# First-block queries and keys projected by tokens, head norms in token layout, convolution taps dealt anew, and the recurrence's constants moved to the start

## The chip, the cores and the metric

The kernel runs on one core of a Trainium2 chip. The metric is the device time of one execution, in microseconds, as the median of several executions. All data is float32. A matrix product is done on TensorE in a rounded 32-bit form (fp32r), with three products for one: each operand is split into a high and a low part.

## The reference

Two transformer blocks over 256 tokens of width 1024, one after the other.

```python
def first_block(x, mem, ...):
    h, mem_h = rms_norm(x, norm_g), rms_norm(mem, mem_norm_g)
    c_glu, c_gate, d_q, d_k, d_v, d_gate, x_q, x_gate, merge = split(h @ w_in)
    y_conv = conformer_conv_branch(c_glu, c_gate, ...)   # 31 taps, layer norm, silu, projection
    y_diff = differential_attention_branch(d_q, d_k, d_v, d_gate, ...)   # 8 heads of 2 x 64
    y_mem = memory_cross_attention_branch(x_q, x_gate, mem_h, ...)       # 4 heads of 256
    g = sigmoid(merge)
    return x + (g[0] * y_conv + g[1] * y_diff + g[2] * y_mem) @ w_out

q = rms_norm(q.reshape(B, S, H, 2, d), qn_g)        # d = 64, over each half head; k likewise
q = rms_norm(q.reshape(B, S, X_HEADS, X_HEAD_DIM), qn_g)   # cross attention, over 256; k likewise
```

The second block has a stick-breaking attention, a gated linear recurrence (its decay needs softplus(-rg_lambda), 512 constants), an output projection, and then the retrieval of experts: for each token and each of 8 heads, 16 of 16384 experts are chosen, two rows of 1024 numbers are fetched for each, and a gelu-weighted sum is made.

## The kernel before, in words

**The work and its order.** Every engine has a program of its own, written out by hand; semaphores tie them together. The weights are read as "slots" of 1024 x 512, listed by weight_slots (line 141): ua0, ub0, ua1, ub1 (the convolution's input), then the 18 slots of the attention stage, q0 k0 v0 q1 k1 v1 xq0 xq1 xk0 xk1 xv0 xv1 m0 to m5, then dg, xg (gates), dp, cg, xp, cp, o (gates and projections), and for the second block xr, q2, k2, g2, v2, w0, w1, pq0. A slot is two pieces of 1 MB. For each piece SP's queue loads w_raw (two buffers, a load waits for the w_lo of the piece two before), ScalarE casts it to w_hi (`hi`, line 879, op on line 885), VectorE subtracts to w_lo (`lo`, line 1500, op on line 1505), and TensorE multiplies. The parts w_hi and w_lo have three buffers, so `hi` runs two pieces ahead of TensorE.

**Two layouts of a product.** `products` (line 414; lines 443 to 445 are the three products hi-hi, lo-hi, hi-lo). By channels the weights stand still in the array and the 256 tokens move: 96 products of 256 columns per slot, the result is channels x tokens. By tokens (token_major) the tokens stand still and 512 channels move: 48 products of 512 columns. Values, merge gates and output projections are by tokens; the queries and keys of the first block are by channels.

**Head norms (q0, k0, q1, k1, xq0, xq1, xk0, xk1).** ScalarE copies the slot from PSUM and squares it (`head_copy`, line 964). TensorE, behind the next slot, sums the squares over each head with a product against ones (`head_sums`, line 483, ops on lines 491 and 497). ScalarE makes Ln and Exp of the whole tile of sums (`head_root`, line 1018, ops on 984 and 994), each with its own table set (`table`, line 874, load on line 876). VectorE multiplies by the gain and the root (`head_scale`, line 1625, op on 1632).

**Attention inside the slots.** In iteration n of the loop over the 18 slots, TensorE does the slot and behind it the pending norm's sums, the values of head n-5, the turn of the probabilities of head n-4 (line 529, waits for VectorE's `diff_probs`, line 1668) and the scores of head n-3 (line 519). VectorE does lo, some taps of the convolution, diff_probs, lo, taps, head_scale, and `diff_tops` (line 1647) of head n-3. In the engine's queue each of these waits for the one before it. Cross attention follows with n-11 to n-13. `turn_input` (TensorE's op is on line 474) turns x, mem, y and b2 by 128x128 transposes against the identity.

**The convolution.** 8 tiles of 128 channels x 31 taps. VectorE has tiles 0 to 2 and the first 23 taps of tile 7 (line 1528), dealt as 3 per piece in the first four attention slots, 2 per piece in the next eight, 4 per piece after, the rest in dg0. GpSimd has tiles 3 to 6 and the last 8 taps of tile 7 (lines 2310 and 2314). `conv_sum` (line 1728) then waits for all of them, `conv_mean` (line 576) sums over channels on TensorE; variance, norm and silu follow while dp0 to cg0 are projected.

**Between the blocks.** After slot o1, VectorE adds the result to x, TensorE turns it (b2), the slot xr is projected, and `spread_scales` (line 654) spreads the tokens' scales. Then comes q2. ScalarE meanwhile issues four small loads for the recurrence and one of 1 MB (the keys), loads a table, and computes exp(-abs(rg_lambda)) (lines 1384, 1386). VectorE computes softplus constants by a series in 18 steps on four elements each (lines 2154 to 2175), before the lo of q2.

**The experts.** From about 600 us on GpSimd issues an indirect load for each of the 256 picks, VectorE makes a dot product (line 1959), ScalarE a scaled identity (line 1229), TensorE adds the row (line 760).

## Time and profile before

| | |
|---|---|
| median of 3 runs | 1256.78 us (1255.48 to 1257.05) |
| the profiled execution | 1257.0 us, its span 1253.6 us |
| TensorE matmuls busy | 1109.1 us (88%), 5044 instructions |
| VectorE busy | 976.4 us (78%), 1972 instructions |
| ScalarE busy | 565.6 us (45%) |
| GpSimd busy | 564.7 us (45%) |
| DMA | 374.27 MB, mean 299 GB/s |

In the profile PE is TensorE's products, PEld its weight loads, DVE VectorE, ACT ScalarE, POOL GpSimd, SP the engine that issues the weight loads; a q behind a name means the engine's sequencer. A row of a timeline is: start in us from the span's start, length in us, engine, line and operation, out<-in, shape, xcount of merged instructions, and in brackets the engine's idle time before it and what ended it. Busy time of TensorE is not the same as speed: its products overlap, so the distance from one start to the next is what one costs.

### The profile page before, as it was taken

To read this page: it belongs to the slowest core of one execution; us is meant where nothing else is said; L and a number is where in the kernel's file an instruction comes from. 1 tells how busy PE (TensorE), PEld (TensorE's weight loads), DVE (VectorE), ACT (ScalarE), POOL (GpSimd) and SP (SyncE) were. 2 spreads that over 40 slices of the span, in tenths; PEclk is the share of its full clock that TensorE was granted. 3 is DMA by queue.
4 is the path that set the end of the run, shared out by engine and by line. 5 is a ranking of instruction groups with operands and counts; after the bars stand their busy time and mean duration, and the time that the engine had idled before them with its cause. 6 is when DMAs were issued, how large, how long until landed. Compare 5 with 4: busy or idle time off the path is not lost.

```text
span 1253.6 us, 14289 instructions
## 1 busy us (share of the span) xinstructions
PE 1109.1 (88%) x5044; PEld 747.1 (60%) x5044; DVE 976.4 (78%) x1972; ACT 565.6 (45%) x1037; POOL 564.7 (45%) x539
## 2 busy tenths in 40 slices
PE   6999999999999998999588987988878897788777
PEld 6989798788999888977343432444324443232222
DVE  5569989998789767687898678886788868787755
ACT  5666768764456444796323333233332333222311
POOL 0099999998320000000444554544544445343432
PEclk9999999999999999999899999999999999999999
DMA  6544333344555554335799999999999999999996
GB/s 245 202 169 158 132 144 139 137 148 153 202 189 181 205 194 171 145 123 227 308 427 427 426 427 427 427 426 427 428 426 427 427 426 424 427 427 423 427 426 272
DMA packets 53943, 374.27 MB, mean 299 GB/s; under 512 B 6896, under 2 KB 6896, under 8 KB 9200
## 3 DMA queue, kind: packets, MB, share of 16 engines
q0 software_dynamic: 37152, 268.45, 50.9%
q1 hardware_dynamic: 14512, 100.67, 22.1%
q10 hardware_dynamic: 2208, 4.24, 1.0%
q8 instruction: 39, 0.64, 0.2%
q14 instruction: 32, 0.26, 0.1%
HBM read 372.29 MB, written 1.05 MB: 298 GB/s over the span
## 4 chain that ended last, share of the span: by engine, by line
PE 44%; DMA 26%; DVE 21%; ACT 5%; issue 3%; POOL 0%; ACTq 0%; POOLq 0%; DVEq 0%; SPq 0%
DMA big<-in_experts,big 11%; PE unit L443 10%; PE unit L444 10%; PE unit L445 10%; PE unit L760 8%; DMA row<-in_experts,big 5%; DMA conv_in<-in_experts,big 5%; DMA work_two<-in_experts,big 4%; DVE w_lo L1505 3%; DVE row L1959 2%; DVE big L1959 2%; DVE big L1865 2%; ACT L876 2%; DVE big L1862 2%; DMA w_raw<-in_weights 1%
## 5 line engine op out<-in xcount | busy, mean ns | idle before, releaser
L1229 ACT ACTIVATE probs<-ident,big 128x128 f32<-128x128 f32 x255 | 102.4, 402 | 430.3 <-DVE big L1969 430.3
L443 PE MATMUL unit<-in_hi,w_hi 128*128 128x256 f32 x800 | 263.3, 329 | 3.9 <-DVE w_lo L1505 3.4
L760 PE MATMUL unit<-row,probs 128*128 128x512 f32 x448 | 215.3, 610 | 44.1 <-ACT probs L1229 43.9
L1505 DVE TENSOR_TENSOR w_lo<-w_raw,w_hi 128x2048 fp32r<-128x2048 f32 x89 | 205.9, 2319 | 54.8 <-ACT w_hi L885 54.5
L444 PE MATMUL unit<-in_lo,w_hi 128*128 128x256 f32 x800 | 226.9, 284 | 0.0
L445 PE MATMUL unit<-in_hi,w_lo 128*128 128x256 f32 x800 | 226.7, 283 | 0.0
L885 ACT CAST w_hi<-w_raw 128x2048 fp32r<-128x2048 f32 x89 | 169.1, 1905 | 96.8 <-PE unit L445 53.4
L760 PE MATMUL unit<-big,probs 128*128 128x512 f32 x344 | 168.4, 619 | 43.6 <-ACT probs L1229 43.5
L2333 POOL DMA_INDIRECT row<-in_experts,big x112 | 133.6, 1193 | 129.0 <-PE unit L760 113.3
L760 PEld LDWEIGHTS unit<-row,probs 128*128 128x128 f32 x448 | 78.2, 190 | 153.9 <-ACT probs L1229 95.3
L443 PEld LDWEIGHTS unit<-in_hi,w_hi 128*128 128x128 f32 x800 | 154.1, 193 | 26.6 <-issue 20.9
L444 PEld LDWEIGHTS unit<-in_lo,w_hi 128*128 128x128 f32 x800 | 154.2, 193 | 20.7 <-issue 20.6
L1959 DVE CUSTOM_DVE_ANT_0 row<-big,row 128x1024 f32<-128x1024 f32 x112 | 136.5, 1219 | 37.9 <-DMA row<-in_experts,big 37.9
L2333 POOL DMA_INDIRECT big<-in_experts,big x85 | 100.7, 1185 | 123.0 <-PE unit L760 108.7
L445 PEld LDWEIGHTS unit<-in_hi,w_lo 128*128 128x128 f32 x800 | 153.9, 192 | 0.0
L760 PEld LDWEIGHTS unit<-big,probs 128*128 128x128 f32 x344 | 60.7, 192 | 132.8 <-ACT probs L1229 87.2
L2314 POOL TENSOR_TENSOR conv_acc<-conv_acc,big 128x256 f32<-128x256 f32 x128 | 133.6, 1044 | 10.7
L1959 DVE CUSTOM_DVE_ANT_0 big<-big 128x1024 f32<-128x1024 f32 x87 | 106.1, 1219 | 35.8 <-DMA big<-in_experts,big 35.8
L2310 POOL TENSOR_SCALAR big<-conv_in,early_small 128x256 f32<-128x256 f32 x128 | 121.1, 946 | 24.6 <-DVE conv_acc L1528 23.9
L443 PE MATMUL unit<-w_hi,in_hi 128*128 128x512 f32 x304 | 120.5, 396 | 1.2 <-ACT work_one L984 1.2
L445 PE MATMUL unit<-w_lo,in_hi 128*128 128x512 f32 x304 | 118.4, 390 | 0.0
L444 PE MATMUL unit<-w_hi,in_lo 128*128 128x512 f32 x304 | 118.4, 389 | 0.0
(313 smaller groups left out, 1617.4 us busy)
## 6 DMA issues: line engine op xcount, KB each, us to landing
w_raw<-in_weights SPq DMA_DIRECT2D x90, 1024.0 KB, 4.8
w_waiting<-in_weights SPq DMA_DIRECT2D x2, 1024.0 KB, 8.1
row<-in_experts,big POOLq DMA_INDIRECT x112, 14.9
big<-in_experts,big POOLq DMA_INDIRECT x89, 13.4
big<-in_x SPq DMA_DIRECT2D x2, 512.0 KB, 5.4
big<-in_mem ACTq DMA_DIRECT2D x1, 1024.0 KB, 4.9
big<-in_x ACTq DMA_DIRECT2D x1, 1024.0 KB, 7.3
big<-in_sub_keys_t ACTq DMA_DIRECT2D x1, 1024.0 KB, 5.9
```

Source lines behind the costliest of these rows:

```text
L443: e.matmul(unit[:, to], *hi_hi, start=first, stop=False)
L444: e.matmul(unit[:, to], *hi_lo, start=False, stop=False)
L445: m = e.matmul(unit[:, to], *lo_hi, start=False, stop=final)
L760: m = e.matmul(unit[:, half * 512:(half + 1) * 512], diag_places[g % 12], UV.ap(g)[:, D + half * 512:D + (half + 1) * 512], start=first, s ...
L876: e.preload_act_table_set(sets[0])
L885: e.copy(split.ap(p)[0][:, :, :], raw.ap(p)[:, :, :]).then_inc(*mark("hi", p))
L1229: e.activation(diag_places[g % 12], ident[:, :], ACT.Copy, scale=here).then_inc(*mark("diag", g))
L1505: e.tensor_tensor(lo_part[:, :, :], raw.ap(p)[:, :, :], hi_part[:, :, :].bitcast(F32), ALU.subtract).then_inc(*mark("lo", p))
L1959: e.tensor_tensor_reduce(out=row_u, in0=h3[:, t, :], in1=row_u, scale=1.0, scalar=0.0, op0=ALU.mult, op1=ALU.add, accum_out=dot[t][:, n:n ...
L2310: e.tensor_scalar(product, src, tap, 1.0, ALU.mult, ALU.mult).then_inc(*mark("pool_product", (t, k)))
L2314: e.tensor_tensor(dst, dst, product, ALU.add).then_inc(*mark("pool_tap", None, *done))
L2333: e.indirect_dma_start(out=UV.ap(g), out_offset=None, in_=experts, in_offset=bass.IndirectOffsetOnAxis(ap=expert[t][:, n:n + 1], axis=0)). ...
```

## The change

1. The eight slots of queries and keys of the first block (BY_TOKENS) are projected by tokens. Their squares are summed per token: for the 64-wide heads ScalarE squares and VectorE reduces, for the 256-wide ones ScalarE squares in four instructions that also sum. ScalarE makes Ln and Exp of 32 or 4 numbers per partition, with the shared table set. VectorE scales the token layout by a broadcast operand. TensorE turns the tile with eight transposes (`head_turn`), behind the next slot, and ScalarE copies it out with the gain (`head_gains`).
2. Taps: tile 7 has 19 taps on VectorE and 12 on GpSimd. VectorE's deal is 3 per piece in the first four attention slots, 1 in the next six, 4 after.
3. exp(-abs(rg_lambda)) and the series stand at the start, behind lambda and the gains and before the first slots. The memset and the four loads of the recurrence's weights stand before the turn of b2, the keys' load behind the copy of the spread scales.
4. conv_sum is behind dp0's first lo, conv_mean on TensorE behind dp0, the variance behind dp1; the layer norm's root is Ln and Exp in place of Sqrt and a reciprocal, and its bias is added on ScalarE.

The diff, cut: the moved blocks of VectorE's program that stay as they were are left out.

```diff
@@ -43,7 +43,7 @@
-SHARED_TILE, SHARED_TAPS = 7, 23
+SHARED_TILE, SHARED_TAPS = 7, 19
@@ -152,10 +152,12 @@
-        add_slots("x", (f"q{i}", "w_in", COL_Q + i * SLOT), (f"k{i}", "w_in", COL_K + i * SLOT))
-        add_slots("x", (f"v{i}", "w_in", COL_V + i * SLOT), token_major=True)
-    add_slots("x", *((f"xq{i}", "w_in", COL_XQ + i * SLOT) for i in range(2)))
-    add_slots("mem", *((f"xk{i}", "w_mem_kv", i * SLOT) for i in range(2)))
+        add_slots("x", (f"q{i}", "w_in", COL_Q + i * SLOT), (f"k{i}", "w_in", COL_K + i * SLOT),
+                  (f"v{i}", "w_in", COL_V + i * SLOT), token_major=True)
+    add_slots("x", *((f"xq{i}", "w_in", COL_XQ + i * SLOT) for i in range(2)),
+              token_major=True)
+    add_slots("mem", *((f"xk{i}", "w_mem_kv", i * SLOT) for i in range(2)),
+              token_major=True)
@@ -354,6 +360,7 @@
+        BY_TOKENS = ("q0", "k0", "q1", "k1", "xq0", "xq1", "xk0", "xk1")
@@ -498,6 +505,18 @@
+            def head_turn(name):
+                src, unit = tm_half(HEAD_NORMS[name][0]), units.take(name + " turn")
+                for wait in W(("scaled heads", name), units.free(name + " turn")):
+                    e.wait_ge(*wait)
+                for j in range(4):
+                    for t in range(TT):
+                        to = j * T + t * P
+                        m = e.transpose(unit[:, to:to + P], src[:, t, j * P:(j + 1) * P],
+                                        ident[:, :])
+                m.then_inc(*mark("turned heads", name))
@@ -774,7 +793,9 @@
                     diff_values(DIFF_HEADS - 1)
-                if pending in HEAD_NORMS:
+                if pending in BY_TOKENS:
+                    head_turn(pending)
+                elif pending in HEAD_NORMS:
                     head_sums(pending)
@@ -793,10 +814,11 @@
                 project(slot[name])
+            project(slot["dp0"])
             conv_mean()
-            project(slot["dp0"])
+            project(slot["dp1"])
             conv_variance()
-            for name in ("dp1", "cg0", "cg1", "xp0", "xp1"):
+            for name in ("cg0", "cg1", "xp0", "xp1"):
                 project(slot[name])
@@ -976,6 +998,54 @@
+            def head_copy_by_tokens(name):
+                dst = tm_half(HEAD_NORMS[name][0])
+                for wait in W(("slot", name)):
+                    e.wait_ge(*wait)
+                e.copy(dst, tm(units.ap(name))).then_inc(
+                    *mark("copied", name, ("unit free", name)))
+                dim = HEAD_NORMS[name][3]
+                before_it = BY_TOKENS.index(name) - 1
+                for wait in W(("copied", name), work.free(name),
+                              ("scaled heads", BY_TOKENS[before_it]) if before_it >= 0 else None):
+                    e.wait_ge(*wait)
+                if dim == DIFF_HEAD_DIM:
+                    e.activation(work.ap(name)[:, :], flat(HEAD_NORMS[name][0]),
+                                 ACT.Square).then_inc(*mark("sq", name))
+                    return
+                head_rms = rms_of_heads[:, 0:2 * TT]
+                for t in range(TT):
+                    for h in range(SLOT // dim):
+                        c = slice(h * dim, (h + 1) * dim)
+                        i = 2 * t + h
+                        a = e.activation(work.ap(name)[:, i * dim:(i + 1) * dim], dst[:, t, c],
+                                         ACT.Square, accum_out=head_rms[:, i:i + 1])
+                a.then_inc(*mark("sq", name, ("work free", name)))
+            def head_roots_by_tokens(name):
+                table(LN_EXP)
+                dim = HEAD_NORMS[name][3]
+                head_rms = rms_of_heads[:, 0:4 * T // dim]
+                for wait in W(("head squares" if dim == DIFF_HEAD_DIM else "sq", name)):
+                    e.wait_ge(*wait)
+                e.activation(head_rms, head_rms, ACT.Ln, bias=EPS6,
+                             scale=1.0 / HEAD_NORMS[name][3]).then_inc(*mark("ln", name))
+                for wait in W(("ln", name)):
+                    e.wait_ge(*wait)
+                e.activation(head_rms, head_rms, ACT.Exp, scale=-0.5).then_inc(
+                    *mark("root", name))
+            def head_gains(name):
+                dst, gain, per_head, _ = HEAD_NORMS[name]
+                unit = tiles4(units.ap(name + " turn")[:, :])
+                for wait in W(("turned heads", name), ("gains", None)):
+                    e.wait_ge(*wait)
+                for j in range(per_head):
+                    a = e.activation(dst[:, j:4:per_head, :], unit[:, j:4:per_head, :], ACT.Copy,
+                                     scale=gain[:, j:j + 1])
+                a.then_inc(*mark("gained", name, ("normed", name),
+                                ("unit free", name + " turn")))
@@ -1245,6 +1315,9 @@
+            e.activation(rg_u, v("rg_lambda_2", 0, RG_TILES), ACT.Abs).then_inc(*mark("act_step"))
+            e.wait_ge(*at(now("act_step"))[1:])
+            e.activation(rg_u, rg_u, ACT.Exp, scale=-1.0).then_inc(*mark("lam_exp"))
@@ -1270,8 +1343,12 @@
+                if pending in BY_TOKENS:
+                    exps.insert(0, partial(head_roots_by_tokens, pending))
...
-                if name in HEAD_NORMS:
+                if name in BY_TOKENS:
+                    head_copy_by_tokens(name)
+                elif name in HEAD_NORMS:
...
@@ -1290,7 +1367,9 @@
                         *mark("merge", i, ("unit free", name)))
-                if pending in HEAD_NORMS:
+                if pending in BY_TOKENS:
+                    head_gains(pending)
+                elif pending in HEAD_NORMS:
                     head_root(pending)
@@ -1314,30 +1393,41 @@
+            for wait in W(("attended", f"x{X_HEADS - 1}")):
+                e.wait_ge(*wait)
+            e.dma_start(x_res, x_in).then_inc(*mark("load_x", "again", ("loaded", "res"), by=16))
+            ahead(slot["dp0"])
...
-            for wait in W(("attended", f"x{X_HEADS - 1}")):
-                e.wait_ge(*wait)
-            e.dma_start(x_res, x_in).then_inc(*mark("load_x", "again", ("loaded", "res"), by=16))
-            hi(slot["dp0"].pieces[0] + 2)
+            hi(slot["dp1"].pieces[0] + 2)
...
-            hi(slot["dp0"].pieces[1] + 2)
-            hi(slot["dp1"].pieces[0] + 2)
-            table(SQRT)
+            hi(slot["dp1"].pieces[1] + 2)
+            hi(slot["cg0"].pieces[0] + 2)
+            rs = work.ap("rs")[:, 0:T]
+            table(LN_EXP)
...
-            e.activation(work.ap("rs")[:, 0:T], units.ap("variance")[:, 0:T], ACT.Sqrt, bias=EPS5,
-                         scale=1.0 / D).then_inc(*mark("root", "rs", ("unit free", "variance")))
-            hi(slot["dp1"].pieces[1] + 2)
-            conv_silu(0)
-            conv_silu(1)
-            ahead(slot["cg0"])
+            e.activation(rs, units.ap("variance")[:, 0:T], ACT.Ln, bias=EPS5,
+                         scale=1.0 / D).then_inc(*mark("ln", "rs", ("unit free", "variance")))
+            for wait in W(("ln", "rs")):
+                e.wait_ge(*wait)
+            e.activation(rs, rs, ACT.Exp, scale=-0.5).then_inc(*mark("root", "rs"))
+            table(EXP_TANH)
+            hi(slot["cg0"].pieces[1] + 2)
+            for half in range(2):
+                for k in range(4 * half, 4 * half + 4):
+                    for wait in W(("conv scaled", k)):
+                        e.wait_ge(*wait)
+                    e.activation(conv_acc[:, k, :], conv_acc[:, k, :], ACT.Identity,
+                                 bias=v("conv_ln_b", k), scale=0.25).then_inc(
+                        *mark("conv_normed", k))
+                conv_silu(half)
@@ -1355,6 +1445,13 @@
             tile_squares_b2(0)
+            for i, w in enumerate((rg_w_a, rg_w_x)):
+                for b in range(2):
+                    for wait in W(("bd zero", None)):
+                        e.wait_ge(*wait)
+                    e.dma_start(bd[i][64 * b:64 * b + 64, :, 64 * b:64 * b + 64],
+                                w.rearrange("(t b) i j -> b i t j", b=2)[b]).then_inc(
+                        *mark(f"load_rg{i}{b}", None, ("bd", i, b), by=16))
             turn_input("b2", "norm_mix_2")
@@ -1394,6 +1475,9 @@
                 *mark("b2 inv", None, ("bank free", "b2 inv")))
+            for wait in W(("y", "cp", 1)):
+                e.wait_ge(*wait)
+            e.dma_start(keys, sub_keys_t).then_inc(*mark("load_keys", None, ("keys", None), by=16))
             hi(piece("k2", 0))
@@ -1635,6 +1719,25 @@
+            def head_squares_by_tokens(name):
+                dim = HEAD_NORMS[name][3]
+                if dim == DIFF_HEAD_DIM:
+                    for wait in W(("sq", name)):
+                        e.wait_ge(*wait)
+                    e.tensor_reduce(rms_of_heads[:, 0:4 * T // dim],
+                                    work.ap(name)[:, :].rearrange("p (i c) -> p i c", c=dim),
+                                    AX, ALU.add).then_inc(
+                        *mark("head squares", name, ("work free", name)))
+            def head_scale_by_tokens(name):
+                dim = HEAD_NORMS[name][3]
+                head_rms = rms_of_heads[:, 0:4 * T // dim]
+                dst = flat(HEAD_NORMS[name][0]).rearrange("p (i c) -> p i c", c=dim)
+                for wait in W(("root", name)):
+                    e.wait_ge(*wait)
+                e.tensor_tensor(dst, dst, head_rms.unsqueeze(2).to_broadcast(
+                    [P, 4 * T // dim, dim]), ALU.mult).then_inc(*mark("scaled heads", name))
@@ -2175,6 +2153,129 @@
...
+                if pending in BY_TOKENS:
+                    head_squares_by_tokens(pending)
+                    norms.insert(0, partial(head_scale_by_tokens, pending))
+                ahead(s, between=norms, convolve=3 if n < 4 else 1 if n < 10 else 4)
+                if pending in BY_TOKENS:
+                    pass
+                elif pending in HEAD_NORMS:
+                    head_scale(pending)
...
+            lo(slot["dp0"].pieces[0] + 2)
+            conv_sum()
+            lo(slot["dp0"].pieces[1] + 2)
+            branch("dp", 0, 1)
...
+            lo(slot["cg0"].pieces[0] + 2)
+            rs = work.ap("rs")[:, 0:T]
+            for k in range(KT):
+                part = conv_acc[:, k, :]
+                for wait in W(("root", "rs")):
+                    e.wait_ge(*wait)
+                e.scalar_tensor_tensor(out=part, in0=part, scalar=v("conv_ln_g", k), in1=rs,
+                                       op0=ALU.mult, op1=ALU.mult).then_inc(
+                    *mark("conv scaled", k, *([("work free", "rs")] if k == KT - 1 else [])))
+            lo(slot["cg0"].pieces[1] + 2)
...
+            turn_input("y", halves=(1,))
+            for wait in W(("y", "cp", 1)):
+                e.wait_ge(*wait)
+            e.memset(gates_w, 0.0).then_inc(*mark("bd zero"))
+            lo(slot["o1"].pieces[0] + 2)
...
```

## Rows read from the trace of the kernel before

**Rows 1.** The page, 40 equal slices of the span, in tenths of busy time
```profile
PE   6999999999999998999588987988878897788777
...
DMA  6544333344555554335799999999999999999996
```

**Rows 2.** Stretches: busy us (count) of PE, PEld, DVE, ACT, POOL; granted clock; DMA share, GB/s
```profile
180.00:200.00 20.00, 20.00 (x160) 19.42 (x160) 18.60 (x24) 14.62 (x28) 19.25 (x21) 1.00 0.30 107
495.60:498.70 3.10, 3.09 (x14) 3.09 (x15) 3.10 (x3) 0.00 (x0) 0.00 (x0) 0.50 0.63 211
640.00:1240.00 600.00, 495.62 (x1294) 215.44 (x1292) 457.27 (x1284) 179.66 (x558) 281.95 (x243) 0.99 1.01 426
```

**Rows 3.** Busy time within slot xq0 (by channels) and xv0 (by tokens)
```profile
145.37:156.98 11.61, 11.61 (x98) 11.61 (x97) 11.44 (x15) 7.00 (x13) 11.11 (x13) 1.00 0.48 157
206.13:217.15 11.02, 11.02 (x50) 9.12 (x49) 10.88 (x15) 8.26 (x15) 10.52 (x12) 1.00 0.36 117
```

**Rows 4.** Timeline of TensorE: two head_sums, and the turn of mem
```profile
171.51 1.89 PE L497 MATMUL unit<-work_two,ones 128*128 128x256 f32 x8
...
186.79 1.89 PE L497 MATMUL unit<-work_two,ones 128*128 128x256 f32 x8
...
85.99 1.91 PE L474 MATMUL unit<-ident,big 128*128 128x128 f32 x16
```

**Rows 5.** Timeline of ScalarE in slot xq1: one of two table loads
```profile
173.83 1.28 ACT L876 ACT_TABLE_LOAD   x1
```

**Rows 6.** Timeline of VectorE, slot xq1 and the scale after it
```profile
160.64 1.49 DVE L1528 SCALAR_TENSOR_TENSOR conv_acc<-conv_in,early_small,conv_acc 128x256 f32<-128x256 f32 x2
162.06 0.94 DVE L1655 SCALAR_TENSOR_TENSOR probs<-early_small,unit 128x768 f32<-128x768 f32 x1
163.03 0.69 DVE L1662 TENSOR_REDUCE col<-probs 128x2 f32<-128x512 f32 x1
...
164.51 2.28 DVE L1505 TENSOR_TENSOR w_lo<-w_raw,w_hi 128x2048 fp32r<-128x2048 f32 x1
...
168.22 0.17 DVE L1675 RECIPROCAL col<-col 128x4 f32<-128x4 f32 x1
...
171.34 2.28 DVE L1505 TENSOR_TENSOR w_lo<-w_raw,w_hi 128x2048 fp32r<-128x2048 f32 x1
...
177.79 1.90 DVE L1632 SCALAR_TENSOR_TENSOR big<-big,col,work_two 128x512 f32<-128x512 f32 x2 [2.68 <-ACT work_two L994]
```

**Rows 7.** Groups of TensorE, 85 to 237 us: busy, mean ns, idle before, releaser
```profile
L443 PE MATMUL unit<-w_hi,in_hi 128*128 128x512 f32 x65 | 25.9, 399 | 1.2 <-ACT work_one L984 1.2
...
L529 PE MATMUL bank<-ident,probs 128*128 128x128 f32 x24 | 4.2, 284 | 2.9 <-DVE probs L1686 2.9
```

**Rows 8.** Timeline of GpSimd: products of the shared convolution tile
```profile
332.39 0.48 POOL L2310 TENSOR_SCALAR big<-conv_in,early_small 128x256 f32<-128x256 f32 x1 [23.89 <-DVE conv_acc L1528]
...
333.79 3.45 POOL L2310 TENSOR_SCALAR big<-conv_in,early_small 128x256 f32<-128x256 f32 x1
```

**Rows 9.** Timeline of TensorE: the start of q2, the first gathered value
```profile
495.61 0.58 PE L443 MATMUL unit<-in_hi,w_hi 128*128 128x256 f32 x1 [3.05 <-DVE w_lo L1505]
...
618.74 2.08 PE L760 MATMUL unit<-conv_in,probs 128*128 128x512 f32 x2 [9.72 <-ACT probs L1229]
```

**Rows 10.** Timeline of VectorE: third w_lo, conv_sum, the recurrence's constants
```profile
23.60 2.29 DVE L1505 TENSOR_TENSOR w_lo<-w_raw,w_hi 128x2048 fp32r<-128x2048 f32 x1 [3.57 <-ACT w_hi L885]
...
353.57 1.22 DVE L1733 TENSOR_TENSOR work_two<-conv_acc 128x1024 f32<-128x1024 f32 x1 [1.20 <-POOL conv_acc L2314]
...
490.15 0.17 DVE L2154 TENSOR_SCALAR col<-col 128x4 f32<-128x4 f32 x1 [5.17 <-ACT col L1386]
...
493.27 2.28 DVE L1505 TENSOR_TENSOR w_lo<-w_raw,w_hi 128x2048 fp32r<-128x2048 f32 x1
```

**Rows 11.** Timeline of ScalarE before q2
```profile
485.02 1.35 ACTq L1375 DMA_DIRECT2D big<-in_rg_w_a  x2
...
490.03 3.68 ACT L885 CAST w_hi<-w_raw 128x2048 fp32r<-128x2048 f32 x2
```

242 lines of the change are left out of this document (101 added, 141 removed).

## The prediction

> **What bounds the kernel now.** I read the page's slices first. They show two regimes: from the second to the nineteenth slice TensorE stands at 8 or 9 and the DMA engines at 2 to 6 tenths; behind it the DMA engines stand at 9 in every slice [rows 1]. The windows confirm it. In the attention stage TensorE is busy for 20.0 of 20 us at the full clock, while 600 us of the expert gathers run at a DMA share of 1.01 and 426 GB/s [rows 2]. So the gather part keeps its length, whatever comes ahead of it: a microsecond taken off the chain before it moves it forward as a whole. Ahead of it TensorE sets the pace, so a removed matmul counts in full if nothing else becomes late. VectorE is the candidate for that: 18.6 of 20 us busy in the same window, 11.44 of 11.61 in one slot [rows 2, 3].
>
> **Part 1, eight slots by tokens.** One slot is 1024x512 weights. By channels it is 96 products of 256 columns and takes 11.61 us; by tokens it is 48 of 512 columns and takes 11.02 us, as xv0 does already [rows 3] (the counts of 98 and 50 take in neighbours at the edges). That is 121 ns against 230 ns for one product: 128 more columns cost nothing extra, but each product carries some 14 ns beyond its columns. 0.59 us x 8 slots = 4.7 us.
> The trace decides this term: with 14 ns a product, halving 96 saves 48 x 14 ns. The Trainium skill (TensorE: Matmul & The Clock Gate, "Wait — 56ns, not 53.3ns?") gives the fixed part of a warm matmul as about 2.5 ns; by that the eight slots would give 8 x 48 x 2.5 ns = 1.0 us, which speaks against the change. The rows show more than that.
>
> **Part 2, sums out, transposes in.** head_sums is two or four fp32 products against ones: 1.89 us to the end of the last [rows 4], some 0.16 us of it a tail that overlaps what follows. head_turn is eight 128x128 transposes; sixteen such, in the turn of mem, take 1.91 with the same tail [rows 4], so eight cost 0.87 us. 0.86 us x 8 = 6.9 us. With part 1, TensorE loses 11.6 us of work.
>
> **Part 3, what the other engines must now do in time.** Per slot ScalarE loses the Ln and Exp of whole tiles and the two table loads of 1.28 us each [rows 5]; Ln, Exp and the recurrence's exponentials share one table set. It gains the square with sums in four pieces (about 2.2 us against 1.06) and a scaled copy of 1024 elements (1.0 to 1.3). I cost it at nothing: it is busy 14.6 of 20 us [rows 2]. VectorE per slot from v1 to xk1: two w_lo of 2.28 that overlap the next by 0.08, taps, diff_tops 2.45 (162.06 to 164.51), diff_probs 3.1 (168.22 to 171.34), head scale 1.9 [rows 6]. Taps fall from four to two (0.71 each: two from 160.64 to 162.06; up to 0.8 elsewhere, I take 0.75), the scale becomes one TENSOR_TENSOR of 1024 elements. Nothing in the trace has its broadcast operand; the plain one is 1.22 [rows 10], the two halves of today's are 1.90 [rows 6]. I take 1.45. For the four 64-wide slots a reduce over 1024 elements is added; 512 take 0.69 [rows 6], so 1.2. Sum: 4.4 + 1.5 + 2.45 + 3.2 + 1.45 = 13.0 us. TensorE's pitch today is 15.28 (from 171.51 to 186.79 [rows 4]), and will be 15.28 - 0.59 - 0.86 = 13.8. It fits, by 0.8 us.
> The order matters more. head_turn waits for the scaled heads behind the next slot. By my schedule ScalarE casts the next w_hi 4.2 us after a slot starts, then come w_lo, a tap and the scale, done at 8.6; TensorE asks at 11.0. diff_probs follows and is done at 12.0; TensorE asks at 12.7. So a steady slot has no wait.
>
> **Part 4, taps dealt anew.** xv0 and xv1 now have eight taps each instead of four, while two differential heads are still running: 3 us more on VectorE, ahead of diff_probs. There TensorE waits about 1.7 and 1.5 us for probs. Other waits that I expect: 1.2 around v0 (ScalarE's unit free, first scale), 0.8 in q1 to v1, 0.3 at m0, 5.5 together. The waits that go are 2.9 for probs and 1.2 for ScalarE's logarithm [rows 7], 4.1. Net -1.4. The shared tile gives GpSimd 12 taps in place of 8: 8 take 21.2 us to the conv_sum that waits for them (332.39 to 353.57 [rows 8, 10]), so 12 take 32 us, to about 353. VectorE's conv_sum is moved behind dp0's first w_lo, about 358, so that nobody waits; today's wait there is 1.20 us of VectorE [rows 10], on no path. The mean, variance and norm of the convolution are reordered and shortened, but the slices show TensorE at 9 from 313 to 470 us [rows 1], and it stays there: nothing.
> Attention: 11.6 - 1.4 = 10.2 us.
>
> **Part 5, recurrence constants ahead.** TensorE waits 3.05 us for q2's w_lo, until 495.61 [rows 9]. VectorE stands behind 3.1 us of four-element steps (490.15 to 493.27 [rows 10]), these behind ScalarE's exponentials, these behind a table load and five DMA issues from 485.02 on; q2's w_hi starts at 490.03 [rows 11]. Now the issues of the recurrence's weights stand in an idle place of ScalarE (before the turn of b2), the keys' issue behind b2_inv's copy, and w_hi comes at 485.0, where the issues begin now; w_lo follows at 487 to 489, 3 us before TensorE is through with xr (495.61 - 3.05 - 0.4 for the spread of the scales). The wait of 3.05 us goes. Behind it the granted clock is 0.50 (1.2 GHz) for 3.1 us [rows 2], and in it 14 products run instead of the 26 of full clock: 1.4 us more. What precedes the fall is that idle time; without it I expect 2.4 GHz. Total 4.4 us. The keys' 1 MB now comes while k2 is loading; w_raw waited anyway, and k2's second piece has some 5 us. In its new place the chain runs from 20.0 to 23.3 us, while VectorE waits for the third w_hi until 23.6 [rows 10]: nothing. Were it on the path it would cost 3.1.
>
> **Sum.** 10.2 + 4.4 = 14.6 us off the profiled execution's 1257.0 (span 1253.6 and 3.4 around it). The median of the runs is 0.2 below that execution: 1242.2.
>
> **Rivals.**
> A (forecast, chance 0.62), between 1236.5 and 1246. The lower end is all removed work and all waits gone: 11.6 + 4.1 + 4.4 = 20.1. The upper is waits twice as long as I think.
> B (0.17): VectorE becomes the bound in attention. It is at 98% in a slot today [rows 3], and its tops, w_lo, scale and probs now hang on ScalarE's w_hi in each slot; if 1.8 us of waiting for w_hi no longer overlaps anything, its slot is 13.0 + 1.8 = 14.8, and six slots lose 1 us each: 8.6 us gained, 1248.
> C (0.09): the wait before q2 is replaced by another (the turn of b2 late behind the DMA issues, or k2's w_lo behind the keys' load), and the clock falls as before: 10.2 gained, 1246.6.
> D (0.06), the other side: the broadcast scale is slow. The loop ScalarE, VectorE, TensorE, ScalarE goes through one instruction that TensorE's queue now waits for, in order, with the scores and the next slot behind it. Its slack is 0.7 us beyond my 1.45. Each further us costs eight us over the slots, and to lose the 14.6 it must take 1.45 + 0.7 + 1.8 = 4 us, twice the highest row (1.90); waits of 3 us would cost clock too. At 4.5 us each it gives 1261. For it: no row has the form. Against it: every VectorE row of 1024 elements lies between 1.2 and 1.9.
> E (0.06): the change gives nothing, because GpSimd's twelve taps end late. From 332 on the same product takes 0.48 or 3.45 us [rows 8], the long ones where a w_lo runs; a mean of 4.5 us per tap in place of 2.65 would end them at 375, conv_sum would hold w_lo behind it some 12 us longer, and the attention gain would be lost: 1254. The Trainium skill (GPSIMD Engine Reference, 1. Specifications) says that GpSimd shares SBUF interfaces with VectorE and contends with its two-input instructions; by that rule, the trace agrees.
>
> **How the numbers follow.** The likeliest is A: 1242. A and B alone hold 0.79; the range 1236.5 to 1250 takes in A, B and C, 0.88, less what lies below A's end. A measurement of this kernel can tell 0.2%, 2.5 us, from no change: faster means below 1254.3. Faster: A, B, C and a little of E, 0.89; same: 0.05, from E and D's mild end; slower: 0.06.
>
> **What would show it.** The windows of xq0 and its like at 11.0 us with 48 products; eight transposes in 0.87 us in place of the sums; scores of xv0 with a wait for probs of 1 to 2 us; no wait before q2 and one level of clock from 13 us to the first gather; the first gathered product 14 to 15 us before 618.74 [rows 9]. I am wrong if the slot pitch in xq0 to xk1 stays above 14.5 us, if waits for scaled heads exceed 1 us, or if the gather part changes its length by over 2 us.

## The result, and the profile after

The kernel before took 1256.9 us (median of four), the changed kernel 1238.53 (1238.16 to 1239.19, four executions): ratio 0.9859, interval 0.9845 to 0.9873. Run once more on another chip it gave 0.9857 (0.9842 to 0.9872); two of the eleven executions of the kernel before beside it took 1575 and 2822 us, far from all others, and are left out. So it is faster by 1.4%, 18 us; the forecast was 1242.0, a gain of 14.6 us, with a range of 1236.5 to 1250.

The profiled execution took 1239.19, its span is 1237.0. The slices of its page (TensorE, its granted clock, the DMA engines), to be laid beside [rows 1]:

```profile
PE   6999999999999999999588887888879888787877
...
PEclk9999999999999999999799999999999999999999
...
DMA  6554434444464655336899999999999999999996
```

The two regimes are there as before; the first one is shorter, and TensorE has no slice under 9 in it behind the first. Four stretches of the changed kernel (busy us and count of PE, PEld, DVE, ACT and POOL, then granted clock, DMA share, GB/s): xq0, which is now by tokens; one whole pitch from xk0 to xk1; q2; and the gather part:

```profile
137.92:148.94 11.02, 11.02 (x51) 9.12 (x50) 10.81 (x15) 5.20 (x10) 10.60 (x12) 1.00 0.54 190
164.74:178.54 13.80, 13.80 (x73) 11.50 (x71) 12.57 (x16) 10.26 (x27) 13.22 (x14) 1.00 0.44 153
...
479.80:491.49 11.69, 11.69 (x98) 11.66 (x97) 10.79 (x19) 4.19 (x3) 0.00 (x0) 1.00 0.56 210
601.82:1237.00 635.18, 523.64 (x1356) 228.09 (x1356) 484.67 (x1360) 188.64 (x586) 293.75 (x251) 0.99 0.99 419
```

A slot that was 11.61 us by channels [rows 3] is 11.02; the pitch fell from 15.28 [rows 4] to 13.80, and TensorE is busy all through it. Between xr and q2 there is no idle time and no clock of 0.50 [rows 2]. The gather part is as long as before (1253.6 - 618.74 = 634.9 [rows 9], now 635.2).

TensorE's waits between 61 and 480 us (what waits, what it waits for, total, times, longest), where before there were 4.1 us in attention [rows 7]:

```profile
PE bank L548 <- DVE probs L1789: 2.2, 3, 1.3
PE unit L450 <- ACT big L1044: 0.7, 1, 0.7
PE unit L481 <- DVE big L2263: 0.5, 1, 0.5
```

2.8 us of these lie in attention: 0.67 ahead of v0, 0.34 behind v1, 0.53 behind xv0, 1.29 behind xv1. The third row is the turn of b2, which waited 0.5 before too.

Since the products' order does not change, every execution can be cut at the same four products: the first of v0, the first of dg0, the end of xr, and the first gathered one. All runs of this study, with their ratio to the kernel before and its interval (the third line, "after again", is the changed kernel on another chip):

| kernel | ratio (interval) | v0 starts | v0 to dg0 | dg0 to end of xr | to first gathered | to end |
|---|---|---|---|---|---|---|
| before | 1 | 89.14 | 229.6 | 173.2 | 126.8 | 634.9 |
| after | 0.9859 (0.9845 to 0.9873) | 86.52 | 219.5 | 173.5 | 122.3 | 635.2 |
| after again | 0.9857 (0.9842 to 0.9872) | 85.32 | 219.6 | 173.5 | 122.1 | 635.2 |
| part 5 undone | 0.9907 (0.9890 to 0.9923) | 86.66 | 219.6 | 173.5 | 126.9 | 634.9 |
| constants late | 0.9875 (0.9858 to 0.9891) | 85.30 | 219.5 | 173.5 | 123.1 | 635.7 |
| issues late | 0.9893 (0.9877 to 0.9910) | 85.17 | 219.6 | 173.6 | 125.1 | 635.2 |
| 16 taps to GpSimd | 0.9873 (0.9857 to 0.9890) | 85.62 | 219.6 | 175.2 | 122.1 | 635.4 |
| by channels, new deal | 0.9989 (0.9980 to 0.9998) | 88.35 | 232.1 | 173.5 | 122.1 | 635.0 |
| by tokens, old deal | 0.9867 (0.9852 to 0.9882) | 85.38 | 221.6 | 173.5 | 122.1 | 635.0 |
| by channels, old deal | 0.9961 (0.9948 to 0.9975) | 88.38 | 229.2 | 173.5 | 122.2 | 634.8 |
| turned twice | 0.9888 (0.9872 to 0.9903) | 85.37 | 223.6 | 173.6 | 122.1 | 634.6 |
| scale 1.3 us later | 0.9940 (0.9927 to 0.9952) | 85.68 | 230.7 | 173.6 | 122.1 | 635.2 |
| even deal | 0.9843 (0.9831 to 0.9856) | 85.48 | 216.8 | 174.7 | 122.5 | 635.1 |
| even deal, w_lo first | 0.9842 (0.9829 to 0.9856) | 85.21 | 218.0 | 173.2 | 122.1 | 635.2 |

The three middle columns repeat within 0.2 us wherever nothing in the stage was touched (once 0.4, the 122.5 of the even deal), the last one within 1.1, while the ratios are good to 0.15%, 1.9 us. So the stages say where, and the ratios that it arrives at the end. The start is less steady: v0 begins 1.2 us later in the first profile of the changed kernel than in the second, where ScalarE had waited less for the weights of its third w_hi (2.79 us and 1.41).

From before to after: 2.6 us until v0 (q0 and k0), 10.1 from v0 to dg0, 4.5 from the end of xr to the first gathered product, -0.3 between, together 16.9.

### The profile page after: what moved, and what is told of

Same layout as the page of the kernel before. It is cut to its first block, busy times and chain, and to the rows that moved or that the text cites. A ratio compares the mean times of both kernels' runs of the same rounds, so it can differ in the third digit from the quotient of the medians.

```text
span 1237.0 us, 13575 instructions
## 1 busy us (share of the span) xinstructions
PE 1097.0 (89%) x4676; PEld 724.1 (59%) x4676; DVE 979.1 (79%) x1960; ACT 549.7 (44%) x1070; POOL 590.0 (48%) x547
## 4 chain that ended last, share of the span: by engine, by line
PE 44%; DMA 25%; DVE 24%; ACT 4%; issue 3%; POOL 0%; POOLq 0%; DVEq 0%; SPq 0%; ACTq 0%
DMA big<-in_experts,big 11%; PE unit L450 10%; PE unit L452 10%; PE unit L451 10%; PE unit L779 9%; DMA row<-in_experts,big 6%; DMA conv_in<-in_experts,big 4%; DVE w_lo L1589 3%; DVE row L2062 3%; DMA work_two<-in_experts,big 2%; DVE big L2062 2%; DVE big L1968 2%; DVE conv_acc L1612 2%; DVE big L1965 2%; DVE big L2072 1%
## 5 line engine op out<-in xcount | busy, mean ns | idle before, releaser
L450 PE MATMUL unit<-in_hi,w_hi 128*128 128x256 f32 x544 | 189.2, 348 | 1.6 <-DVE in_lo L1676 0.9
L450 PE MATMUL unit<-w_hi,in_hi 128*128 128x512 f32 x432 | 171.0, 396 | 0.7 <-ACT big L1044 0.7
L451 PE MATMUL unit<-w_hi,in_lo 128*128 128x512 f32 x432 | 168.3, 390 | 0.0
L452 PE MATMUL unit<-w_lo,in_hi 128*128 128x512 f32 x432 | 168.3, 390 | 0.0
L451 PE MATMUL unit<-in_lo,w_hi 128*128 128x256 f32 x544 | 153.7, 283 | 0.0
L452 PE MATMUL unit<-in_hi,w_lo 128*128 128x256 f32 x544 | 153.6, 282 | 0.0
L2411 POOL TENSOR_SCALAR big<-conv_in,early_small 128x256 f32<-128x256 f32 x132 | 136.6, 1035 | 3.5 <-DVE conv_acc L1612 2.5
L450 PEld LDWEIGHTS unit<-in_hi,w_hi 128*128 128x128 f32 x544 | 104.2, 191 | 23.0 <-issue 20.5
L451 PEld LDWEIGHTS unit<-in_lo,w_hi 128*128 128x128 f32 x544 | 104.1, 191 | 20.5 <-issue 20.3
L452 PEld LDWEIGHTS unit<-in_hi,w_lo 128*128 128x128 f32 x544 | 104.0, 191 | 0.0
```

The source lines that it names most:

```text
L450: e.matmul(unit[:, to], *hi_hi, start=first, stop=False)
L451: e.matmul(unit[:, to], *hi_lo, start=False, stop=False)
L452: m = e.matmul(unit[:, to], *lo_hi, start=False, stop=final)
L2411: e.tensor_scalar(product, src, tap, 1.0, ALU.mult, ALU.mult).then_inc(*mark("pool_product", (t, k)))
```

## Experiments: the recurrence's part

**Part 5 undone.** Two groups of lines stand again where they stood, between the scales of b2's tokens and the cast for q2 on ScalarE, and between b2's reciprocal and q2's w_lo on VectorE. The arithmetic, cut:

```diff
+            table(LN_EXP)
+            e.activation(rg_u, v("rg_lambda_2", 0, RG_TILES), ACT.Abs)
+            e.activation(rg_u, rg_u, ACT.Exp, scale=-1.0)
...
+            e.tensor_scalar(rg_z, rg_u, 2.0, None, ALU.add)
...
+            e.scalar_tensor_tensor(out=neg4sp, ...)
```

and the issues, four for the weights and one for the keys, with the memset that they wait for:

```diff
+            e.memset(gates_w, 0.0)
...
+            e.dma_start(bd[i][64 * b:64 * b + 64, :, 64 * b:64 * b + 64], ...)
+            e.dma_start(keys, sub_keys_t)
```

> The changed kernel (1238.5 us) with the whole of part 5 undone: ScalarE's two exponentials with their table load, VectorE's chain of four-element steps, the memset, the four loads of the recurrence's weights and the keys' load all stand where they stood before, between the scales of b2's tokens and the casts for q2. Theory (part 5, 4.4 us): +4.4 us, 1242.9; TensorE waits about 3.0 us ahead of q2 and its granted clock stands at 0.5 for some 3 us behind that wait. Rival 1, the stage gained something else than this wait (another overlap of b2's turn or of k2's load): under 1 us, 1239.5 or less. Rival 2, the clock has nothing to do with the wait: +3.0 us, the clock at 1.0.

Ratio 0.9907 against 0.9859 and 0.9857. The stage from the end of xr is 126.9 us in place of 122.1 to 122.3, 4.6 to 4.8 more. TensorE's timeline (start, duration, what it does, idle time before), and the window behind the wait:

```profile
483.45 0.57 PE L450 MATMUL unit<-in_hi,w_hi 128*128 128x256 f32 x1 [3.04 <-DVE w_lo L1592]
```

```profile
483.45:486.45 3.00, 3.00 (x14) 3.00 (x15) 3.00 (x3) 0.00 (x0) 0.00 (x0) 0.51 0.67 216
```

The wait is back at its old length (3.05 [rows 9]), and so are 14 products in 3 us at 1.2 GHz: the theory's 4.4, and neither rival. The next two runs show that the length of the stage hangs on VectorE all the same.

**Only the constants late**: the first of the two diffs alone, the issues and the memset early.

> Of part 5 only the arithmetic is undone: the exponentials with their table load and VectorE's chain stand late again, the DMA issues and the memset stay early. Worked out from the changed kernel's trace: the cast for q2 starts 1.7 us later (472.1 to 473.8), the chain of 3.1 us begins at 474.0 and ends at 477.1, w_lo at 479.3, and TensorE asks for it at 479.8. Theory: no wait, 0 to +0.3 us; the two halves of part 5 cost only together, each alone fits into the 3.5 us by which w_lo is early. Rival 1, the chain on VectorE is the cost: +3 us, and the clock falls. Rival 2, costs simply add (half of 4.4 each): about +2.

q2 starts 0.25 us behind the end of xr, as in the changed kernel: no wait, the clock at 1.0. VectorE's chain ran from 472.76, its second w_lo ended at 480.4. But the stage is 0.8 to 1.0 us longer than in the changed kernel; it comes in later, as a wait of 1.9 us ahead of L640 (1.07 there), the first product of the second block's stick-breaking attention that needs logarithms made by ScalarE and VectorE. So the wait before q2 was judged rightly, and "nothing" was wrong by a microsecond that I had no term for. The trace has it: behind q2's two w_lo VectorE scales the slot xr, and that is now late. The row in the changed kernel (its second profile, where xr ends at 478.43), and in this one (xr ends at 478.30):

```profile
479.54 1.23 DVE L1706 TENSOR_TENSOR conv_in<-unit,work_one 128x1024 f32<-128x1024 f32 x1 [2.10 <-ACT work_one L1476]
...
480.31 1.21 DVE L1709 TENSOR_TENSOR conv_in<-unit,work_one 128x1024 f32<-128x1024 f32 x1
```

It starts 1.11 us behind the end of xr in the one, 2.01 in the other.

**Only the issues late**: the second diff alone, the constants early.

> Of part 5 only the issues are undone: the memset, the four loads of the recurrence's weights and the keys' load stand late again, ahead of the cast for q2; the constants stay early. Worked out: the issues wait for the memset until 472.5 and take 3.3 us, the cast ends at 477.6, w_lo at 479.9, TensorE asks at 479.8. Theory: +0.1 us (0 to 0.5). Rival 1, the transfers themselves (1.5 MB between the weights of q2 and k2) hold up weights: +2 us or more, with waits for raw weights. Rival 2, costs simply add: about +2.

Theory missed: 125.1, 2.9 to 3.0 us more. ScalarE and its queue, and what TensorE does at q2 and at L640:

```profile
471.41 1.35 ACTq L1465 DMA_DIRECT2D big<-in_rg_w_a  x2
472.79 1.30 ACTq L1465 DMA_DIRECT2D big<-in_rg_w_x  x2
474.13 1.57 ACTq L1470 DMA_DIRECT2D big<-in_sub_keys_t  x1
476.10 1.90 ACT L907 CAST w_hi<-w_raw 128x2048 fp32r<-128x2048 f32 x1 [5.07 <-issue]
```

```profile
480.38 0.38 PE L450 MATMUL unit<-in_hi,w_hi 128*128 128x256 f32 x1 [1.42 <-DVE w_lo L1589]
...
538.53 0.67 PE L640 MATMUL unit<-work_one,later 128*128 128x512 f32 x1 [2.15 <-issue]
```

I had taken the keys' issue at 0.6 us, as it was before; here it took 1.57, and w_lo came 1.4 us too late. The lateness turns up a second time at L640, and there it is larger than TensorE's own. VectorE's scale of xr starts 4.10 us behind the end of xr here and 5.72 with the whole of part 5 undone. Against the 1.11 of the changed kernel that is 0.9, 3.0 and 4.6 us later in the three runs, and the stage is 1.0, 3.0 and 4.8 longer. All of VectorE's later work moves with it: its next idle time ends 20.80, 22.82 and 24.44 us behind the end of xr, in the changed kernel 19.85. TensorE's own delay ahead of q2 was none, 1.4 and, with the clock, 4.4. So the length of the stage follows VectorE's queue behind q2's w_lo and not TensorE's wait ahead of q2; TensorE has a wait at L640 in every kernel (0.94 with part 5 undone, 1.92 and 2.15 with one half of it). Rival 1, the transfers, does not explain the loss: ScalarE did wait 4.96 us for the raw weights of k2's first cast (0.55 in the changed kernel), but VectorE had no idle time from the first w_lo of q2 to the w_lo of k2. The clock stayed at 1.0 behind both waits. Each half of part 5 therefore costs something alone (0.9 and 2.9), and both together 4.7, a microsecond more than their sum: not the sharp "only together" of my theory, and not two equal halves either. Most of it hangs on the issues, not on the arithmetic. I can't say why the keys' issue takes 0.35 us in the changed kernel and 1.57 here.

## Experiments: tokens and taps

**By channels again**, all else as in the changed kernel; **the old deal of taps** alone; and **both undone**:

```diff
-        add_slots("x", (f"q{i}", ...), (f"k{i}", ...), (f"v{i}", ...), token_major=True)
+        add_slots("x", (f"q{i}", ...), (f"k{i}", ...))
+        add_slots("x", (f"v{i}", ...), token_major=True)
...
-        BY_TOKENS = ("q0", "k0", "q1", "k1", "xq0", "xq1", "xk0", "xk1")
+        BY_TOKENS = ()
```

```diff
-SHARED_TILE, SHARED_TAPS = 7, 19
+SHARED_TILE, SHARED_TAPS = 7, 23
-   ahead(s, between=norms, convolve=3 if n < 4 else 1 if n < 10 else 4)
+   ahead(s, between=norms, convolve=3 if n < 4 else 2 if n < 12 else 4)
```

> The changed kernel with parts 1 and 2 undone: the eight slots by channels again, norms by head_sums with Ln, Exp and the two-piece scale; the new deal of taps, the early constants and the later mean stay. Theory (TensorE is the bound, removed work counts in full): 8 x 0.59 us of products and 8 x 0.86 us of sums come back, 11.6 us; the waits stay about those of the changed kernel (2.8 us). dg0 starts 11 to 13 us later than in the changed kernel (at 306 there), the whole is 10.5 to 13 us longer. Rival 1, VectorE had set the pace before and the gain came from its relief: then 2 taps per slot with the old norm give most of it, and the kernel is under 8 us longer. Rival 2, the fixed part of a product is small (a rule of the Trainium skill gives 1.0 us for part 1): some 8 us.

> The changed kernel with the old deal of taps: 23 of the shared tile on VectorE, 3, 2 and 4 per piece (by tokens, transposes, early constants and later mean stay). Theory: VectorE's work per slot from v1 to xk1 rises by two taps, 13.0 to 14.5 us, above TensorE's 13.8; six slots lose 0.7 us each (4.2), and the waits of xv0 and xv1 (0.5 and 1.3) go: +2.4 us (1 to 4), pitch of xk0 to xk1 at 14.5 in place of 13.8. Rival 1, the deal does nothing for the time: 0, pitch 13.8. Rival 2, the idle time of VectorE in these slots can't be used, since it comes ahead of w_hi: +6 or more, pitch above 15.

> The changed kernel with both undone, slots by channels and the old deal: what is left of the change is the recurrence's constants and issues ahead and the later mean. Theory: the gain of these alone is the 4.4 us of part 5; the attention stage is that of before (dg0 some 12.7 us later than in the changed kernel, waits of 4.1 us in attention), 4.4 us faster than before: ratio 0.9965. Rival 1, the later mean, variance and norm are worth something too: 6 us or more off before. Rival 2: part 5 is worth nothing without the rest: ratio 1.

From v0 to dg0: by tokens 219.6 with the new deal, 221.6 with the old; by channels 232.1 with the new and 229.2 with the old. Both undone give before's stage (229.6) and 0.9961, where 0.9965 was expected: parts 1, 2 and the deal make the attention's gain, part 5 the rest, the later mean nothing (173.5 against 173.2 us from dg0 to the end of xr).

By channels alone costs more than the 10.5 to 13 us expected: with the 2.7 us of q0 and k0 it is 15.2 us, counted from q0's first product. The work that comes back is 11.6; the rest is waits (5.5 us for probs in place of 2.2, and 1.2 ahead of v0 in place of 0.7):

```profile
PE bank L546 <- DVE probs L1787: 5.5, 3, 3.3
PE unit L448 <- ACT work_one L1052: 1.2, 1, 1.2
```

So a deal is good for one form and bad for the other: the new one gains 2.0 us by tokens and loses 2.9 by channels. By tokens the old deal lengthens the pitch of xk0 as worked out, from 13.80 to 14.55 (166.44 to 180.99; 14.5 expected). The windows of the two slots behind it, xk1 (13.87 in the changed kernel) and xv0 (14.61 there), with VectorE busy for 28.45 of 28.87 us:

```profile
180.99:195.32 14.33, 14.07 (x73) 11.53 (x72) 14.12 (x18) 10.12 (x25) 13.83 (x15) 1.00 0.42 147
195.32:209.86 14.54, 14.04 (x73) 11.54 (x72) 14.33 (x18) 10.52 (x22) 13.96 (x15) 1.00 0.44 145
```

But the loss is not 0.7 us in each of six slots: it is 1.1 in k1 and 1.3 in v1, 0.7 and 0.5 in xk0 and xk1, 0.3 in xq0 and xq1 together, and xv1 is 1.5 shorter. The total of 2.0 beside 2.4 expected comes out of another sharing-out.

**The transposes issued twice**, to see whether TensorE is the bound:

```diff
-                for j in range(4):
+                for j in range(8):
+                    j = j % 4
```

> The changed kernel with the eight transposes of head_turn issued twice in each of the eight slots (64 transposes more, the same result). Theory (TensorE is the bound through attention): each slot with a turn is 0.87 us longer, 7.0 us in all, less what waits absorb (those of xv0 and xv1, 1.8 us, hang on VectorE and shrink): +5.5 to +7, pitch of xk0 to xk1 at 14.7 in place of 13.8. Rival B, VectorE or the loop through ScalarE sets the pace: under +3, pitch 13.8 to 14.2.

The pitch of xk0 is 14.68 and that of xk1 14.74, TensorE busy through both: the theory's 14.7. From v0 to dg0 it is only 4.0 us more for 6.1 us of work (seven of the eight turns), and nothing more until v0, where q0's turn took the place of the wait. That is under the 5.5 to 7 expected: the waits for probs shrank from 2.2 to 0.6 us and that at v0 went.

```profile
166.42:181.10 14.68, 14.68 (x81) 12.38 (x80) 12.63 (x16) 10.38 (x26) 14.10 (x15) 1.00 0.48 164
181.10:195.84 14.74, 14.74 (x81) 12.38 (x80) 12.29 (x15) 10.37 (x26) 14.24 (x15) 1.00 0.41 140
```

```profile
PE bank L549 <- DVE probs L1790: 0.6, 1, 0.6
```

TensorE bounds the steady slots; the remaining waits for probs are VectorE's, and more work on TensorE hides them. A wait costs some 0.2 us more than the idle time shown for it: with and without one of 0.53 us xv0 takes 14.61 and 13.87 us (the even deal, below).

**The scale later and dearer**, which puts rival D to the test (cut):

```diff
+                e.tensor_tensor(dst, dst, dst, ALU.max)...
+                e.wait_ge(...)
                 e.tensor_tensor(dst, dst, head_rms..., ALU.mult)
```

> The changed kernel with one more TENSOR_TENSOR of 1024 elements (a maximum of the heads with themselves, which changes nothing) on VectorE directly ahead of the broadcast scale, in each of the eight slots: the scale is 1.3 us later and VectorE has 1.3 us more to do per slot. This takes the place of rival D's slow scale, at 2.5 us instead of 1.2. Theory: VectorE's slot grows from 13.0 to 14.3 us, 0.5 above TensorE's 13.8; in all +4 us from q0 to dg0 (3 to 6), pitch of xk0 to xk1 at 14.3. Rival 1, VectorE's idle time in these slots (0.9 us) and the 0.7 us of slack take nothing up: +8 us or more. Rival 2, plenty of room: under 1 us.

Rival 1: 11.1 us more from v0 to dg0 (10.4 us on the median, 1248.28 against 1237.91 for the changed kernel on the same chip). The waits; the windows ahead of and behind the end of the longest; and a third window, behind another wait:

```profile
PE bank L548 <- DVE probs L1791: 5.1, 4, 2.2
PE unit L516 <- DVE big L1740: 4.7, 3, 2.9
PE bank L579 <- DVE probs L1817: 0.7, 1, 0.7
```

```profile
98.00:99.70 1.70, 0.00 (x0) 0.00 (x0) 1.67 (x3) 0.00 (x0) 1.62 (x2) 0.84 0.33 135
99.70:101.30 1.60, 1.58 (x8) 1.59 (x9) 1.60 (x1) 0.00 (x0) 1.60 (x2) 0.50 0.00 0
131.00:133.00 2.00, 2.00 (x6) 1.62 (x5) 1.93 (x4) 0.00 (x0) 1.92 (x4) 0.50 0.85 238
```

Waits of 10.5 us stand in attention in place of 2.8, 7.7 more, and twice the clock falls to 1.2 GHz: the eight transposes at 99.7 take 1.97 us in place of 1.04. The steady slots I had looked at took it up nearly whole: 0.26 us of waiting between 145 and 200 us, pitches of 14.34, 14.11 and 13.84. The loss is in the others: 2.89 for k0's scaled heads behind v0, where VectorE has six taps and the reduce as well, 2.17 for the first probs behind k1, 0.98 and 1.68 behind xv0, 0.98 behind xv1, and less behind k0 (0.87, ahead of v0) and m0 (0.72).

**GpSimd late**, which puts rival E to the test:

```diff
-SHARED_TILE, SHARED_TAPS = 7, 19
+SHARED_TILE, SHARED_TAPS = 7, 15
```

> The changed kernel with SHARED_TAPS 15 in place of 19: GpSimd gets 16 taps of the shared tile, VectorE four fewer. This makes rival E true on purpose. Worked out from the changed kernel's trace: 16 taps of 2.7 us from about 322 end at 365.5; conv_sum, which ends at 360.5 now, ends at 367.9; the mean's two products, which TensorE starts at 363.0, wait 4.9 us; behind so long a wait the clock falls as it did ahead of q2 before (3 us at 0.5, 1.4 us). Theory: +6.3 us, 1244.8 (4 to 7). Rival 1, w_lo and the mean have enough room: 0. Rival 2, the wait without a fall of the clock: +4.9. Rival 3: GpSimd's taps get faster when VectorE does less beside them, so that the wait is half as long: +2.

The theory (6.3 us) missed: it is 1.6 us more from dg0 to the end of xr. GpSimd's first tap of the shared tile, VectorE's conv_sum, and TensorE's first product of the mean:

```profile
319.45 0.48 POOL L2411 TENSOR_SCALAR big<-conv_in,early_small 128x256 f32<-128x256 f32 x1 [0.38 <-DVE conv_acc L1612]
```

```profile
361.26 1.22 DVE L1836 TENSOR_TENSOR work_two<-conv_acc 128x1024 f32<-128x1024 f32 x1 [3.93 <-POOL conv_acc L2415]
```

```profile
363.73 0.48 PE L599 MATMUL unit<-work_two,ones 128*128 128x256 f32 x1 [1.33 <-DVE work_two L1842]
```

Sixteen taps took 41.8 us (319.45 to 361.26), 2.61 each: the first twelve 2.77 each (to 352.74), no faster than the changed kernel's twelve (2.73, 32.8 us from 322.17, and 2.86 in its second profile), the last four 2.1. They began 2.7 us sooner, 2.0 if counted from dg0, because GpSimd had been waiting for VectorE's last shared tap. The changed kernel:

```profile
322.17 0.48 POOL L2411 TENSOR_SCALAR big<-conv_in,early_small 128x256 f32<-128x256 f32 x1 [2.47 <-DVE conv_acc L1612]
...
323.57 3.45 POOL L2411 TENSOR_SCALAR big<-conv_in,early_small 128x256 f32<-128x256 f32 x1
```

So the conv_sum started at 361.26 in place of the 365.5 worked out, and of 3.9 us of VectorE's waiting 1.3 reached TensorE. The clock stayed at 1.0. Rival 3 has the size nearly right and the reason for the most part wrong: 2.0 us is the sooner start, 1.4 the mean of 2.61 in place of the 2.7 that I took, which only the last four taps bring. The change had 2 to 3 us of room here (GpSimd done at 354.92, conv_sum at 358.13; in the second profile 355.38 and 357.45). That a tap's product takes 0.48 us or, beside a w_lo, 3.45 is unchanged. The Trainium skill (GPSIMD Engine Reference, 1. Specifications) says that GpSimd shares its SBUF interfaces with VectorE and contends with VectorE's instructions that have two inputs in SBUF. The trace agrees, with these two lengths.

## Experiments: a better deal

**The even deal**: two taps a piece in xv0 and xv1, the eight left over in dg0 and dg1, the shared tile's taps among the others.

```diff
-   ahead(s, between=norms, convolve=3 if n < 4 else 1 if n < 10 else 4)
+   ahead(s, between=norms, convolve=3 if n < 4 else 1 if n < 10 else 2 if n < 12 else 4)
-   taps += [(k, SHARED_TILE) for k in range(SHARED_TAPS)]
+   taps = [(k, t) for k in range(CONV_K) for t in range(KT)
+           if t not in POOL_TILES or t == SHARED_TILE and k < SHARED_TAPS]
-   convolve_some(len(taps))
...
-   ahead(slot["dg1"])
+   ahead(slot["dg1"], convolve=4)
+   convolve_some(len(taps))
```

> The changed kernel with another deal of the same 112 taps of VectorE: two per piece instead of four in xv0 and xv1, the eight taps so freed in dg0 and dg1, and the taps of the shared tile among the others rather than behind them. Theory (the waits of 0.5 and 1.3 us for probs in xv0 and xv1 come from the eight taps in each of these slots): both go, q0 to dg0 takes 242.9 us, 1.8 us less, and GpSimd no longer waits 2.5 us for the shared tile, so that conv_sum keeps its place at 356 to 358 us: 0.9985 of the changed kernel. Rival 1, the waits have another cause (ScalarE's exponentials, the chain of probs itself): under 0.5 us. Rival 2, the taps left for dg0 and dg1 make w_lo late there: the gain is given back between dg0 and dp0.

Both waits went, 2.8 us less from v0 to dg0 (1.8 expected: xv0 and xv1 are 2.2 us shorter, m0 0.4), and GpSimd has no wait for a shared tap. Then 1.2 us came back, ahead of xp0, a place that neither account named; TensorE, then VectorE:

```profile
395.48 0.50 PE L450 MATMUL unit<-w_hi,in_hi 128*128 128x512 f32 x1 [1.23 <-DVE w_lo L1589]
```

```profile
390.75 1.21 DVE L1823 SCALAR_TENSOR_TENSOR work_two<-work_two,unit 128x1024 f32<-128x1024 f32 x1
391.99 1.23 DVE L1828 TENSOR_TENSOR conv_acc<-conv_acc,work_two 128x1024 f32<-128x1024 f32 x1
393.14 2.28 DVE L1589 TENSOR_TENSOR w_lo<-w_raw,w_hi 128x2048 fp32r<-128x2048 f32 x1
```

TensorE is 2.6 us earlier by the clock of the trace than in the changed kernel's second profile, but conv_sum only 1.3 (356.16 against 357.45). GpSimd is not the reason: its last tap ended at 352.70, and conv_sum waited for nothing. It stands behind a w_lo, this behind a cast, and this behind its weights, as does the cast ahead of the norm's table load:

```profile
352.02 1.90 ACT L907 CAST w_hi<-w_raw 128x2048 fp32r<-128x2048 f32 x1 [2.43 <-DMA w_raw<-in_weights]
...
372.77 1.91 ACT L907 CAST w_hi<-w_raw 128x2048 fp32r<-128x2048 f32 x1 [3.20 <-DMA w_raw<-in_weights]
```

In the changed kernel ScalarE waited there for TensorE's products (up to 3.9 us at a time, between 350 and 375) and not for weights. The norm's steps run on ScalarE and VectorE behind the second of these casts and ahead of the w_lo of xp0; VectorE's gate operation ahead of it starts at 390.75 (392.18 in the changed kernel, 1.4 earlier). What brings the weights no sooner I have not followed further; a load waits for a w_lo, and a 1 MB load of x is issued at 348.57.

**And that w_lo ahead of cg0's two gate operations:**

```diff
-            gate_slot("cg0", ...)
-            ahead(slot["cg1"])
+            lo(slot["cg1"].pieces[0] + 2)
+            gate_slot("cg0", ...)
+            lo(slot["cg1"].pieces[1] + 2)
```

> The kernel with the even deal, and on VectorE the first w_lo of cg1's turn (the one that xp0's first piece needs) moved ahead of cg0's two gate operations. With the even deal alone q0 to dg0 took 242.05 us, 2.8 less than in the changed kernel, but 1.2 of it came back as a wait of 1.23 us for that w_lo ahead of xp0 (TensorE asked at 394.25; the gate operations ran from 390.75 to 393.1 and w_lo behind them, while its w_hi was done at 390.3). Theory: w_lo is then done at about 393, the wait goes, from dg0 to the end of xr it takes 173.5 us again instead of 174.7, and the kernel is 1.2 us shorter than with the even deal alone: ratio to before 0.983. Rival 1, the next w_lo or the unit of cg0, freed 2.3 us later, makes a wait in xp0 or xp1 of the same size: no gain. Rival 2, the w_lo is late for lack of its w_hi, not behind the gate: no gain, the wait stays at 1.2.

The wait ahead of xp0 went, 173.2 us in place of 174.7; the first gathered product starts at 598.51 (599.45 with the even deal alone, 600.52 and 601.82 in the changed kernel). In this execution a wait for probs of 0.86 us stood in q1 to v1, which the even deal alone didn't have. Medians: 1236.0 and 1236.22, beside 1237.91 for the changed kernel in the even deal's own comparison. The two ratios (0.9842, 0.9843) can't be told apart, and against the changed kernel's 0.9857 their intervals overlap. By the stages, from v0 to the first gathered product, they are 1.2 and 1.9 us shorter; the times of the whole agree with that and don't prove it.

## Why the prediction was right, and which term was mis-sized

In attention it was right by the mechanism of case A, in part 5 by the size alone. By its own steps:

- **Part 1** (4.7 us): 11.02 us for each slot, as taken. The prediction's "128 more columns cost nothing extra" is a slip: 256 more columns cost 109 ns, and 0.59 us over 48 products is 12 ns of fixed part for one, not 14; the sum used the 0.59. The Trainium skill (TensorE: Matmul & The Clock Gate, "Wait — 56ns, not 53.3ns?") gives a warm product's fixed part, back to back, as about 2.5 ns. By an estimate from that figure a slot would have kept 11.5 us (11.61 less 48 x 2.5 ns); the trace differs, with 11.02. Each product here has a weight load of its own.
- **Part 2** (6.9 us): eight transposes from 161.92 to the next product at 162.80, 0.88 us (0.87 taken). Turned twice, the pitch grew by that again.
- **Part 3** (VectorE 13.0 us beside 13.8): right in the steady slots, where VectorE is busy for 12.6 and 13.2 us of a pitch of 13.80 and 13.87 and no turn waits for its scaled heads. So rival B did not come. The broadcast scale is as dear as a plain one, mostly: its group, with the mean of all eight, is

```profile
L1738 DVE TENSOR_TENSOR big<-big,col 128x1024 f32<-128x1024 f32 x8 | 11.9, 1486 | 0.0
```

  1.49 us against the 1.45 taken; single ones 1.21 to 1.76.
- **Part 4** (waits that come, 5.5 us): this is the mis-sized term. They were 2.8: 0.67 at v0 (1.2 expected), 0.34 from q1 to v1 (0.8), 0.53 and 1.29 in xv0 and xv1 (1.7 and 1.5), none at m0 (0.3). Attention gave 12.7 us in place of 10.2. (The upper end of case A, "waits twice as long", adds up to 1247.7 and not 1246; nothing hangs on it.) The cause named for xv0 and xv1, eight taps in each, is shown by the even deal, without which they wait and with which they don't. GpSimd's twelve taps ended at 355 (353 expected), and conv_sum started at 358.13 with no wait (358), so rival E did not come.
- **Part 5** (4.4 us): 4.5 measured, 4.6 to 4.8 when undone. The size is right, the path is not. The prediction added TensorE's wait ahead of q2 (3.05) and the clock behind it (1.4). Both did go. But the stage ends when VectorE's and ScalarE's work behind q2's w_lo is through. VectorE was 4.6 us late there, so the agreement with 4.4 is in part luck, and the two halves tell the accounts apart: with the issues alone late TensorE lost 1.4 us ahead of q2 and the stage 3.0, with the constants alone late none and 1.0. A delay of TensorE alone, with VectorE on time, no run shows. The account made for the runs, that the five issues and the chain hurt only together, fell with it. At the start the chain costs nothing, as said: v0 starts at 85.32 in the changed kernel's second profile, and at 85.30 with the constants late.
- **Two of the signs** did not come as written. The clock does not stand at one level until the first gather: in the 7.8 us without a product ahead of the gathered ones it is at 1.2 GHz, as it was before:

```profile
594.00:601.80 7.80, 0.00 (x0) 0.00 (x0) 7.52 (x22) 4.12 (x8) 6.58 (x5) 0.50 1.01 413
...
612.00:618.70 6.70, 0.00 (x0) 0.00 (x0) 6.56 (x17) 3.13 (x7) 5.78 (x4) 0.50 1.01 424
```

  (the first row is the changed kernel's, the second that of before). And the first gathered product comes 16.9 us sooner, not 14 to 15. Of [rows 1] the prediction says that the DMA engines stand at 9 in every slice behind the nineteenth; the next one has 7 and the last 6.
- **The gather part**: 635.2 against 634.9, as said. In all the runs it lies between 634.6 and 635.7 while its start moves by 20 us.
- **Around the span** the profiled execution of before had 3.4 us, that of the changed kernel 2.2. The sum kept 3.4. Another execution of before took 1255.17 with a span of 1253.0, 2.2 around it: the 3.4 belonged to that one execution. From profiled execution to profiled execution the gain is 17.8: the 14.6 of the sum, 2.5 for the waits that did not come, 1.2 around the span, less some 0.5 in the other stages.

**Rival D** was priced far too low. I gave the scale a slack of 0.7 us and then a price of a microsecond per slot, so that it had to take 4 us to undo the change. With 2.8 us (1.48 for the maximum and 1.34 for the scale, mean of eight) in place of 1.49 it took back 11 of the 17. The slack came from a steady slot, xq0 to xk1, and the trace bears it out there. But q0, k0, v0 and q1 have three taps per piece, k0, v0, k1 and v1 have the reduce as well (by the prediction's own terms 13.0 + 1.2 = 14.2 us in v1, beside a pitch of 13.8), and xv0 and xv1 have eight taps each. VectorE had no room in these already in the changed kernel; slots q1 and v1:

```profile
98.31:110.25 11.94, 11.94 (x60) 9.62 (x58) 11.94 (x11) 5.88 (x5) 11.52 (x10) 1.00 0.52 179
...
123.55:137.92 14.37, 14.03 (x73) 11.53 (x72) 14.16 (x17) 10.34 (x20) 13.79 (x15) 1.00 0.42 147
```

Two of the waits that came there are long enough to be followed by a fall of the clock. The chance of 0.06 was spent on the wrong question: how dear the instruction is, not how little room the other slots leave.

## What to carry to other kernels

When an engine's work is made shorter, deal the other engines' filler work anew with it: here the same deal was worth 2 us with one form of the slots and cost 3 with the other. Take the slack of a loop from its tightest round, not from a typical one, and price a wait with the clock that may fall behind it. A wait that goes is not yet the gain: ask which engine's chain ends the stage (here VectorE's queue behind q2's w_lo, and not TensorE's wait ahead of q2). A gain in an early stage is kept only as far as the other engines' chains (here the casts that wait for weights, and the norm behind them) move forward with it; cut the traces at the same instructions and compare the stages, which repeat to 0.2 us here where whole times repeat to 2.

## What the runs showed of the hardware

- The clock doesn't fall behind every wait of a given length: it fell to 1.2 GHz behind waits of 3.04 and 2.89 us, and between 129 and 131 us, behind one of 2.17 us that had ended at 128.1, but stayed at 2.4 GHz after one of 3.29 us (by channels with the new deal, in xv1), one of 2.15 (the issues late, at L640) and those of 1.3 to 1.9.
- The issue of the same 1 MB load on ScalarE's queue took 0.35 us in the changed kernel, 0.61 before and with all of part 5 undone, and 1.57 with the issues alone late.
- A TENSOR_TENSOR of 1024 elements with a broadcast second operand costs what the plain one does: 1.21 us at least and 1.76 at most in the changed kernel, mean 1.49; the plain maximum in the same place took 1.21 to 1.76, mean 1.48.
